# Both feed-forward down products: seven block products for eight in chunks of four K tiles, all low halves on GpSimd

## The chip, the cores and the metric

The kernel runs on one core of a Trainium2 chip. The metric is device time in microseconds of that core, from launch to end, as the median of several executions. Lower is better.

## The reference, cut to what matters

Two transformer-like blocks are applied to one sequence of 1024 tokens with 1024 features, all in fp32. Each block ends in a feed-forward. Only the two down projections matter here:

```
# first block: D_FF = 2816, 22 K tiles of 128
f = (gelu(gate) * val) @ w_down          # [1024, 2816] @ [2816, 1024]
h = h + rms_norm(f, ln_ffn_post)
# second block: D_FF_2 = 4096, 32 K tiles of 128
x = x + square(relu(h2 @ w_up_2)) @ w_down_2   # [1024, 4096] @ [4096, 1024]
return rms_norm_2(x, final_norm_2)
```

## The kernel before

Every fp32 product is made of three matmuls in TensorE's fp32r type. Each operand is rounded to a high half (ScalarE, `activation` Copy), the rest is taken as a low half (raw minus high, a `tensor_tensor` on GpSimd or VectorE), and TensorE adds high x high, high x low and low x high in PSUM. The low half is written over the raw data.

Five programs, one for each engine (SP issues the DMAs), are written out by hand in order. An engine runs its list strictly in order; semaphores hold it where it needs another's result. The class `Steps` (L107) numbers the steps of a repeated part, so that `wait(eng, name, j)` waits for step `name` of round `j`.

**First down product** (channels on the partitions, result `y[:, m, :]`, m = 0 to 7). It goes in 11 chunks of two K tiles. For each chunk SP loads 1 MB of `w_down` (L2612) and 1 MB of the stored activations (L2624), ScalarE rounds (L2633), GpSimd makes the low halves (L2646; those of the first activations are made by VectorE, L2659), TensorE makes 96 matmuls of 128x512 (`down_products`, L2670: eight output rows m, two PSUM banks each, two rows in flight), and VectorE adds each PSUM result to `y` (`add_one`, L2994; chunk 0 is copied by ScalarE, L2665). Three SBUF homes for chunks (L211) let the loads run ahead. The last chunk also feeds the sums of squares of the norm behind it.

**Second down product** (tokens on the partitions). It goes in 16 chunks of two K tiles in the same way (L2763, L2782, L2791, `token_products` L2691). `token_add` (L2723) scales each PSUM result by a per-token factor and adds it to `y` in one `scalar_tensor_tensor`. Behind chunks 0 and 1, TensorE transposes four residual tiles each into PSUM (L2705) and VectorE adds them (L2715). In the last chunk each output row is normed and stored.

Seven-product stages exist already in both up projections and in part of the second block's input projection (`r7_products`, L3128, called "ring" and "pair" stages): the two operands are cut into quadrants, VectorE makes the sums of quadrants, and seven block products replace eight. Those stages write their low halves on VectorE. SP, GpSimd, ScalarE, TensorE and VectorE reach the two down products in their programs at L3343 to L3356 and L3448 to L3462, L3539 to L3545 and L3570, L3664 to L3682 and L3785 to L3793, L3849 to L3852 and L3905 to L3912, L4027 to L4031 and L4161 to L4167.

Of the kernel before, what the change touches and what calls it, by code (L numbers as in the profile page):

```python
# [15 lines left out]
P = 128  # L16
T = 1024
# [61 lines left out]
DOWN1 = FF_TILES // 2  # L79
DOWN2 = FF2_TILES // 2  # L80
# [4 lines left out]
PRODUCT_OPENS = [True, True, False, True, False, False, False]  # L85
TILE_ORDER = [0, 4, 1, 5, 2, 6, 3, 7]
# [19 lines left out]

class Steps:  # L107
# [3 lines left out]
    def __init__(self, sem, names):  # L111
        self.sem, self.names, self.at = sem, names, 0
        self.index = {name: k for k, name in enumerate(names)}
        assert len(self.index) == len(names)

    def start(self, eng):
        eng.sem_inc(self.sem, len(self.names))
# [6 lines left out]
    def wait(self, eng, name, j):  # L124

        eng.wait_ge(self.sem, j * len(self.names) + (len(self.names) + self.index[name] + 1))
# [6 lines left out]
    def wait_iterations(self, eng, j):  # L133

        eng.wait_ge(self.sem, j * len(self.names) + len(self.names))


def build_program(nc, a, out):
    ctx = ExitStack()
    with ctx:  # L140
# [87 lines left out]
        token_sq = at("token_sq", 32, [P, D])  # L228
# [15 lines left out]
        def x7_hi_at(i, b0, b1):  # L244
            if len(x7_hi[i]) == 1:
# [22 lines left out]
        f2h = [[at("f2h_00", 76, [P, T], F32R), at("f2h_01", 88, [P, T], F32R)],  # L268
               [at("f2h_10", 168, [P, T], F32R), at("f2h_11", 172, [P, T], F32R)]]
        f2l = [at("f2l_0", 80, [P, 2, T], F32R), at("f2l_1", 160, [P, 2, T], F32R)]  # L270
        f2raw = [at("f2raw_0", 80, [P, 2, T]), at("f2raw_1", 160, [P, 2, T])]
        d2raw = [at("d2raw_0", 176, [P, 2, D]), at("d2raw_1", 152, [P, 2, D])]
        d2h = [at("d2h_0", 184, [P, 2, D], F32R), at("d2h_1", 144, [P, 2, D], F32R)]
        d2l = [at("d2l_0", 176, [P, 2, D], F32R), at("d2l_1", 152, [P, 2, D], F32R)]
# [354 lines left out]
        pre_sum = Steps(sem("pre_sum"), ["css", "cp"])  # L629
# [6 lines left out]
        sc_act = Steps(sem("sc_act"), ["tA0", "tA1"])  # L636
        sc_dve = Steps(sem("sc_dve"), ["SB00", "SB01", "SB10", "SB11", "SN0", "SN1"])
# [16 lines left out]
        out_pe = Steps(sem("out_pe"), ["tY0", "tY1", "gate0", "gate1"])  # L654
        out_act = Steps(sem("out_act"), ["square", "root", "ln0", "ln1", "hi"])
        out_dve = Steps(sem("out_dve"), ["sum", "mean", "center", "var", "rr", "norm", "gate0", "gate1"])
        out_pool = Steps(sem("out_pool"), ["lo"])
# [1950 lines left out]
        def down_home(c):  # L2608

            return 2 - c % 2 if c else 0  # L2610
# [1584 lines left out]
```

## Time and profile before

| what | value |
| --- | --- |
| time, median of 3 runs | 3028.42 us (3022.24 to 3031.68) |
| span of the profiled execution, first to last instruction | 3028.7 us |
| own time of that execution | one of the three runs' times; the page gives only its span |
| TensorE matmuls | 2909.7 us, 96% of the span |
| VectorE | 1822.3 us, 60% |
| ScalarE | 1191.0 us, 39% |
| GpSimd | 538.9 us, 18% |
| mean granted TensorE clock | 0.988 |

In the profile PE is TensorE, PEld its weight load, DVE VectorE, ACT ScalarE, POOL GpSimd, SPq the DMA queue of SP. L480 is the line of the matmuls of all three-matmul products outside the seven-product stages. A group's busy time adds the durations of its instructions. A matmul is shown with its whole length (389 ns), while the next starts before it ends, so the pace of matmuls is read from the length of a stretch and its count. "Idle before" says for what the engine waited before the instruction.

### The profile page before, as it was taken

How to read it: one execution, taken by the hardware profiler on the slowest of the kernel's cores; microseconds unless marked ns; L12 is line 12 of the kernel's file. 1: busy time of each engine (PE TensorE's matmuls, PEld its weight loads, DVE VectorE, ACT ScalarE, POOL GpSimd, SP SyncE). 2: the span in 40 equal slices, each digit the busy share in tenths (PEclk: the TensorE clock that was granted, in tenths of full speed). 3: DMA queues.
4: the chain of work that ended last, by engine and by line, in shares of the span. 5: the costliest groups of instructions: out<-in, count | busy, mean ns of one | idle time of the engine just before them, and what ended most of it. 6: DMA issues, size and time to landing. Idle time of an engine off the chain costs nothing.

```text
span 3028.7 us, 47692 instructions
## 1 busy us (share of the span) xinstructions
PE 2909.7 (96%) x20002; PEld 2338.6 (77%) x20002; DVE 1822.3 (60%) x2306; ACT 1191.0 (39%) x1769; POOL 538.9 (18%) x228
## 2 busy tenths in 40 slices
PE   8999988889899999999899999999899999999999
PEld 6877777777688888888688767666688888878887
DVE  3156778741799889444885455555456655554445
ACT  4155545632645555321543343444334333221112
POOL 3310122221100000444141200000021000043342
PEclk9999999999999999999999999999899999999999
DMA  6433430002422222322444634444544333342322
GB/s 210 152 114 112 126 114 25 27 32 78 159 70 84 84 84 77 133 111 84 132 149 147 208 105 126 147 135 136 195 132 132 105 112 111 125 160 84 112 84 111
DMA packets 252247, 350.09 MB, mean 116 GB/s; under 512 B 11377, under 2 KB 187642, under 8 KB 252034
## 3 DMA queue, kind: packets, MB, share of 16 engines
q1 hardware_dynamic: 237058, 299.85, 31.0%
q10 hardware_dynamic: 14976, 47.19, 4.1%
q8 instruction: 159, 2.61, 0.4%
q14 instruction: 54, 0.44, 0.0%
HBM read 238.17 MB, written 108.82 MB: 115 GB/s over the span
## 4 chain that ended last, share of the span: by engine, by line
PE 87%; DVE 5%; issue 3%; DMA 2%; ACT 2%; SPq 1%; POOL 0%; DVEq 0%; ACTq 0%
PE ps L480 36%; PE ps L3159 17%; PE ps L2929 10%; PE ps L2095 5%; PE ps L664 4%; PE ps L1512 4%; PE ps L2146 2%; PE ps L2165 2%; PE ps L2123 1%; PE ps L1575 1%; PE ps L2126 1%; DMA kl<-qk_lo 1%; PE ps L1553 0%; PE ps L506 0%; PE ps L2131 0%
## 5 line engine op out<-in xcount | busy, mean ns | idle before, releaser
L446 POOL TENSOR_TENSOR wl<-wraw,wh 128x1024 fp32r<-128x1024 f32 x62 | 157.2, 2537 | 1118.0 <-ACT wh L441 1108.4
L2734 DVE SCALAR_TENSOR_TENSOR y<-ps,token_s,y 128x1024 f32<-128x1024 f32 x120 | 154.0, 1284 | 164.1 <-PE ps L480 164.0
L480 PE MATMUL ps<-xh,wh 128*128 128x512 f32 x752 | 237.9, 398 | 5.4 <-DVE yb L1318 1.4
L480 PE MATMUL ps<-xl,wh 128*128 128x512 f32 x752 | 233.7, 392 | 0.0
L480 PE MATMUL ps<-xh,wl 128*128 128x512 f32 x752 | 233.2, 391 | 0.0
L441 ACT ACTIVATE wh<-wraw 128x1024 fp32r<-128x1024 f32 x78 | 82.4, 1058 | 268.1 <-PE ps L480 206.4
L480 PEld LDWEIGHTS ps<-xh,wh 128*128 128x128 f32 x752 | 139.8, 190 | 47.2 <-issue 9.4
L2996 DVE TENSOR_TENSOR y<-ps,y 128x1024 f32<-128x1024 f32 x79 | 96.8, 1225 | 125.6 <-PE ps L480 125.6
L2795 POOL TENSOR_TENSOR d2l<-d2raw,d2h 128x2048 fp32r<-128x2048 f32 x16 | 74.0, 4624 | 520.8 <-ACT d2h L2786 520.8
L480 PEld LDWEIGHTS ps<-xl,wh 128*128 128x128 f32 x752 | 142.4, 189 | 30.3
L480 PEld LDWEIGHTS ps<-xh,wl 128*128 128x128 f32 x752 | 142.3, 189 | 30.2
L480 PE MATMUL ps<-d2h,f2h 128*128 128x512 f32 x512 | 157.9, 389 | 0.0
L480 PE MATMUL ps<-d2l,f2h 128*128 128x512 f32 x512 | 157.6, 389 | 0.0
L480 PE MATMUL ps<-d2h,f2l 128*128 128x512 f32 x512 | 157.6, 389 | 0.0
L2359 DVE CUSTOM_DVE_ANT_0 pbuf<-ps,bias 128x640 f32<-128x640 f32 (+7 forms) x128 | 85.7, 706 | 99.5 <-PE ps L2131 47.2
L2650 POOL TENSOR_TENSOR d1l<-d1raw,d1h 128x2048 fp32r<-128x2048 f32 x11 | 50.9, 4627 | 490.8 <-ACT d1h L2639 490.8
L2786 ACT ACTIVATE d2h<-d2raw 128x2048 fp32r<-128x2048 f32 x16 | 30.7, 1921 | 255.4 <-DMA d2raw<-in_w_down 253.0
L3244 DVE SCALAR_TENSOR_TENSOR cb<-ub,cols,cb 128x1024 f32<-128x1024 f32 x88 | 112.5, 1299 | 5.1 <-ACT cb L3227 3.5
L480 PEld LDWEIGHTS ps<-d2l,f2h 128*128 128x128 f32 x512 | 96.1, 188 | 20.1
L480 PEld LDWEIGHTS ps<-d2h,f2h 128*128 128x128 f32 x512 | 96.1, 188 | 20.0
L480 PEld LDWEIGHTS ps<-d2h,f2l 128*128 128x128 f32 x512 | 96.1, 188 | 19.9
L2275 ACT ACTIVATE pt<-ps 128x512 f32<-128x512 f32 (+2 forms) x96 | 44.3, 465 | 166.8 <-PE ps L2146 166.8
(487 smaller groups left out, 7477.3 us busy)
## 6 DMA issues: line engine op xcount, KB each, us to landing
wraw<-in_w_in SPq DMA_DIRECT2D x48, 512.0 KB, 4.9
r_raw<-in_w_up SPq DMA_DIRECT2D x38, 512.0 KB, 3.8
residual<-src ACTq DMA_DIRECT2D x32, 512.0 KB, 5.0
w_raw<-in_w_up SPq DMA_DIRECT2D x32, 512.0 KB, 5.1
act_d<-act SPq DMA_DIRECT2D x32, 512.0 KB, 6.2
d2raw<-in_w_down SPq DMA_DIRECT2D x16, 1024.0 KB, 5.0
f2raw<-act_d SPq DMA_DIRECT2D x16, 1024.0 KB, 7.1
proj<-stage SPq DMA_DIRECT2D x30, 512.0 KB, 3.1
```

The lines of the kernel that those rows point to most:

```text
L441: nc.scalar.activation(wh[:, s, :, :], wraw[:, s, :, :], ACT.Copy).then_inc(w_hi, 1)
L446: nc.gpsimd.tensor_tensor(wl[:, s, :, :], wraw[:, s, :, :], wh[:, s, :, :].bitcast(F32), ALU.subtract).then_inc(w_lo, 1)
L480: mm = nc.tensor.matmul(ps[:, bank + h, :], w, x[:, h * HALF:(h + 1) * HALF], start=start and k == 0, stop=stop and k == 2)
L664: return nc.tensor.matmul(to, left, right, **kw)
L1512: ins = mm(ps[:, 2 * fill_slot(u) + h, :], w[:, s, kt, :], x[:, kt, h * HALF:(h + 1) * HALF], start=kt == 0 and part == 0, stop=kt == KT - ...
L2095: ins = mm(ps[:, 6 + h, :], w[:, s, kt, :], x[:, kt, h * HALF:(h + 1) * HALF], start=kt == 0 and part == 0, stop=kt == KT - 1 and part == 2)
L2359: a2_dve.done(nc.vector.tensor_tensor_reduce(pbuf[:, step % 3, m, 0:size], ps[:, 2 * m:2 * m + 2, :].rearrange("p a n -> p (a n)")[:, 0:size],
L2734: ins = nc.vector.scalar_tensor_tensor(out=y[:, m, :], in0=bank2(2 + m % 2), scalar=token_s2[:, m:m + 1], in1=y[:, m, :], op0=ALU.mult, op ...
L2929: mm = nc.tensor.matmul(ps[:, bank, :], w, x, start=PRODUCT_OPENS[b] and i == 0 and k == 0, stop=i == 3 and k == 2, skip_group_check=True)
L2996: nc.vector.tensor_tensor(y[:, m, :], bank2(2 + m % 2), y[:, m, :], ALU.add).then_inc(down_added, 1)
L3159: mm = nc.tensor.matmul(ps[:, bank, :], w, x, start=PRODUCT_OPENS[b] and i == 0 and k == 0, stop=i == 3 and k == 2, skip_group_check=True)
L3244: ff1_dve.done(nc.vector.scalar_tensor_tensor(out=cb[:, r, :], in0=ub[:, r, 2 - back:T + 2 - back], scalar=col("conv_w", (2 - back) * 2 * ...
```

## The change

The first down product becomes: two chunks of two K tiles as before (tiles 0 to 3), four chunks of four K tiles (tiles 4 to 19) with seven block products each, and one chunk of two (tiles 20 and 21). The second becomes: three chunks of two (tiles 0 to 5), six of four (6 to 29), one of two (30 and 31). Both residual turns move one chunk later.

A chunk of four K tiles is loaded as eight quarters of 512 KB. VectorE makes eight sums of two quarters each (128x1024). There are then seven left and seven right operands; ScalarE rounds each into a ring of three (first product) or four (second) slots, and GpSimd makes each of the fourteen low halves in place. TensorE makes 24 matmuls for each of seven block products, in four PSUM banks, alternating between the lower and upper four. Where `PRODUCT_OPENS` is false, a block product is accumulated on what the same four banks hold already. After each block product VectorE adds the four banks to one quadrant of `y`, in two halves: one 128x1024 `tensor_tensor` for a half in the first product, two 128x512 `scalar_tensor_tensor` in the second.

```diff
+DOWN1_TILES = [0, 2, 20]
+DOWN2_TILES = [0, 2, 4, 30]
+SUMS = {"T1": ("B3", "B12", "B0"), "S3": ("A4", "A0", "A21"), "T2": ("B2", "B5", "B3"), "T3": ("B4", "B5", "B12"),
+        "S1": ("A3", "A21", "A6"), "S2": ("A2", "A3", "A0"), "T4": ("B6", "B1", "B2"), "S4": ("A5", "A1", "A2")}
...
+        seven1 = Seven(0, 4, 4, lambda k, half: quarter_of(a["w_down"], k, half),
+                       lambda k, half: quarter_d(act1_d, k, half), *homes1, 3, False)
+        seven2 = Seven(4, 6, 6, lambda k, half: quarter_d(act2_d, k, half),
+                       lambda k, half: quarter_of(a["w_down_2"], k, half), *homes2, 4, True)
...
+        def seven_load(sp, g, e):
+            j, k, raw = g.first + e, g.tile0 + 4 * e, g.raw[e % 2]
+            if e:
+                d7_sum.wait(sp, "S1", j - 1)
+            if e >= 2:
+                d7_pe.wait(sp, "01", j - 2)
+            load("B0", g.right, 0, 0, 0)
+            load("B12", g.right, 0, 1, 0)
+            load("A0", g.left, 0, 0, 1)
+            load("A21", g.left, 0, 1, 1)
+            if e >= 2:
+                d7_pe.wait(sp, "11", j - 2)
+            load("B1", g.right, 1, 0, 2)
+            load("A1", g.left, 1, 0, 2)
+            if e >= 2:
+                d7_pe.wait(sp, "51", j - 2)
+            load("B5", g.right, 1, 1, 3)
+            if e >= 2:
+                d7_pe.wait(sp, "61", j - 2)
+            load("A6", g.left, 1, 1, 3)
...
+        def seven_round(act, g, e, b):
+            if b == 0:
+                d7_sum.wait(act, "S4", j)
+            if at_ >= g.ring:
+                d7_pe.wait(act, f"{(at_ - g.ring) % 7}1", g.first + (at_ - g.ring) // 7)
+            for x in "AB":
+                d7_hi.done(nc.scalar.activation(g.high[x][at_ % g.ring][:, :, :], g.raw[e % 2][f"{x}{b}"][:, :, :], ACT.Copy),
+                           f"{x}{b}")
...
+        def seven_lows_pool(pool, g, e):
+            for b in range(7):
+                seven_rest(pool, g, e, "A", b)
+                seven_rest(pool, g, e, "B", b)
...
+        def seven_products(pe, g, e):
+            for b in range(7):
+                d7_low.wait(pe, f"B{b}", j)
+                for h in range(2):
+                    if b >= 2:
+                        d7_add.wait(pe, f"{b - 2}{h}", j)
+                    elif e:
+                        d7_add.wait(pe, f"{b + 5}{h}", j - 1)
+                    for i in (2 * h, 2 * h + 1):
+                        for kt in range(2):
+                            for k, (w, x) in enumerate(((a_hi, b_hi), (a_hi, b_lo), (a_lo, b_hi))):
...
+        def seven_adds(dve, g, e, b):
+            for h in range(2):
+                d7_pe.wait(dve, f"{b}{h}", j)
+                if g.scaled:
+                    for i in range(2 * h, 2 * h + 2):
+                        ins = nc.vector.scalar_tensor_tensor(out=y[:, m, part], in0=ps[:, bank + i, :],
+                                                             scalar=token_s2[:, m:m + 1], in1=y[:, m, part],
+                                                             op0=ALU.mult, op1=ALU.add)
+                else:
+                    ins = nc.vector.tensor_tensor(to, ps[:, bank + 2 * h:bank + 2 * h + 2, :], to, ALU.add)
...
+        def seven_dve(dve, g):
+            names = list(SUMS)
+            for e in range(g.chunks):
+                for b in range(7):
+                    if e + 1 < g.chunks:
+                        if b < 4:
+                            seven_sums(dve, g, e + 1, names[2 * b:2 * b + 2])
+                    if b:
+                        seven_adds(dve, g, e, b - 1)
+                    elif e:
+                        seven_adds(dve, g, e - 1, 6)
+            seven_adds(dve, g, g.chunks - 1, 6)
... SP
+            seven_load(sp, seven1, 0)
             load_w(sp, U_FA, 0, w_cols(a["w_in_2"], FA_COL))
             load_w(sp, U_QKV2, 1, w_cols(a["w_in_2"], 0))
...
+            sp.wait_ge(down_done, 2 * KT)
+            for e in range(1, seven1.chunks):
+                seven_load(sp, seven1, e)
... VectorE, first product
+            p7_pe.wait(dve, "P4", F1_PAIRS - 1)
+            seven_sums(dve, seven1, 0, SUMS)
             dve.wait_ge(down_added, KT)
...
+            seven_dve(dve, seven1)
... VectorE, second product
+            for c in range(3):
                 for m in range(TT):
                     token_add(dve, c, m)
+                    if c == 1:
+                        seven_sums(dve, seven2, 0, list(SUMS)[m:m + 1])
... TensorE, first product
+            for c in range(2):
+                down_products(pe, c)
+            pe.wait_ge(down_added, 2 * KT)
+            for e in range(seven1.chunks):
+                seven_products(pe, seven1, e)
```

In the programs of ScalarE and GpSimd, the first chunk's rounding of the first product waits for down chunk 0 to be through TensorE, that of the second for token chunk 1. The two `wl` low halves that GpSimd makes for the next stage (L446) stand behind seven-chunk 1. In the second product SP issues the first chunk's eight quarters ahead of the residual's reload, and TensorE waits for the last residual addition and the last token addition before the first block product.

## Rows read from the trace of the kernel before

**Rows 1.** the page: busy time of each engine, share of the span; then the chain's shares.

```profile
PE 2909.7 (96%) x20002; PEld 2338.6 (77%) x20002; DVE 1822.3 (60%) x2306; ACT 1191.0 (39%) x1769; POOL 538.9 (18%) x228
...
PE 87%; DVE 5%; issue 3%; DMA 2%; ACT 2%; SPq 1%; POOL 0%; DVEq 0%; ACTq 0%
PE ps L480 36%; PE ps L3159 17%; PE ps L2929 10%; PE ps L2095 5%; PE ps L664 4%; PE ps L1512 4%; PE ps L2146 2%; PE ps L2165 2%; PE ps L2123 1%; PE ps L1575 1%; PE ps L2126 1%; DMA kl<-qk_lo 1%; PE ps L1553 0%; PE ps L506 0%; PE ps L2131 0%
```

**Rows 2.** chain that ended last, in time (start us, us, what), first down product.

```profile
1189.96 24.04 PE ps L3159 x106
...
1223.47 236.94 PE ps L480 x1044
1460.48 1.10 issue
```

**Rows 3.** the same chain, second down product.

```profile
2663.01 21.82 PE ps L480 x96
...
2689.81 21.83 PE ps L480 x96
...
2716.61 304.70 PE ps L480 x1344
...
3021.34 1.30 DVE y L2734
```

**Rows 4.** GpSimd in order of time (start us, us, instruction), chunk 4 of the first.

```profile
1295.78 4.63 POOL L2650 TENSOR_TENSOR d1l<-d1raw,d1h 128x2048 fp32r<-128x2048 f32 x1 [12.17 <-ACT d1h L2639]
1300.38 4.76 POOL L2656 TENSOR_TENSOR f1l<-f1raw,f1h 128x1024 fp32r<-128x1024 f32 x2
1305.10 4.74 POOL L446 TENSOR_TENSOR wl<-wraw,wh 128x1024 fp32r<-128x1024 f32 x2
```

**Rows 5.** one line's instructions: count, duration min/median/max in ns, first and last start.

```profile
L2996 DVE TENSOR_TENSOR y<-ps,y x79: 1224/1225/1225, 1248.3 to 1460.4; 128x1024 f32<-128x1024 f32 x79
...
L2734 DVE SCALAR_TENSOR_TENSOR y<-ps,token_s,y x120: 1277/1284/1285, 2692.6 to 3021.3; 128x1024 f32<-128x1024 f32 x120
...
L3191 DVE TENSOR_TENSOR ub<-r_u,r_m x19: 678/683/686, 875.8 to 1223.9; 128x512 f32<-128x512 f32 x19
...
L3193 DVE TENSOR_TENSOR ub<-ps,r_u x19: 680/693/693, 876.7 to 1224.4; 128x512 f32<-128x512 f32 x19
```

**Rows 6.** GpSimd and VectorE in order of time, where both read SBUF at 1216 us.

```profile
1216.50 4.61 POOL L2650 TENSOR_TENSOR d1l<-d1raw,d1h 128x2048 fp32r<-128x2048 f32 x1 [374.23 <-ACT d1h L2639]
...
1217.47 5.85 DVE L2663 TENSOR_TENSOR f1l<-f1raw,f1h 128x1024 fp32r<-128x1024 f32 x2 [4.60 <-ACT f1h L2644]
1223.25 0.68 DVE L3189 TENSOR_TENSOR ub<-ps,r_m 128x512 f32<-128x512 f32 x1
1223.85 0.68 DVE L3191 TENSOR_TENSOR ub<-r_u,r_m 128x512 f32<-128x512 f32 x1
...
1225.16 2.36 DVE L3204 TENSOR_TENSOR ub<-ub,rstd 128x1024 f32<-128x1024 f32 x2
```

**Rows 7.** the two engines again, 1523 to 1531 us.

```profile
1520.31 4.46 POOL L446 TENSOR_TENSOR wl<-wraw,wh 128x1024 fp32r<-128x1024 f32 x1
1524.79 4.39 POOL L2341 TENSOR_TENSOR ls<-st,hs 128x1024 fp32r<-128x1024 f32 x1
...
1522.42 1.19 DVE L2064 SCALAR_TENSOR_TENSOR st<-ps,rstd 128x1024 f32<-128x1024 f32 x1
1523.54 7.79 DVE L3033 TENSOR_TENSOR t_raw<-y,t_raw 128x2048 f32<-128x2048 f32 x2
```

**Rows 8.** a group of ScalarE's: busy us, mean ns of one.

```profile
L2644 ACT ACTIVATE f1h<-f1raw 128x1024 fp32r<-128x1024 f32 x20 | 20.1, 1053 | 7.6 <-DMA f1raw<-act_d 7.6
```

**Rows 9.** SP's DMA issues in order of time; GB/s in 40 slices of 2663:2690.

```profile
1234.17 0.33 SPq L3260 DMA_DIRECT2D act_d<-fout  x1
...
1267.31 0.37 SPq L2620 DMA_DIRECT2D d1raw<-in_w_down  x1
...
GB/s 0 115 97 400 431 407 401 267 267 194 279 328 419 431 413 413 437 413 376 376 431 401 431 431 401 425 425 413 395 419 425 407 188 49 97 309 449 407 407 449
```

**Rows 10.** the page: a 512 KB load's time from issue to landing.

```profile
proj<-stage SPq DMA_DIRECT2D x30, 512.0 KB, 3.1
```

**Rows 11.** stretches: busy us (x count) by engine, PEclk, DMA share, GB/s.

```profile
1733.50:1737.50 4.00, 0.58 (x3) 0.19 (x3) 1.23 (x1) 0.00 (x0) 0.00 (x0) 1.00 1.07 373
1738.00:1741.40 3.40, 3.40 (x13) 2.74 (x11) 0.00 (x0) 1.06 (x1) 1.33 (x1) 0.53 0.90 278
```

More of the change, by code:

```diff
@@ L104, with __init__, final @@
     t7: int
+@dataclass
+class Seven:
+    first: int
+    chunks: int
+    tile0: int
+    left: object
+    right: object
+    raw: list
+    low: list
+    high: dict
+    ring: int
+    scaled: bool
 class Steps:
-    def __init__(self, sem, names):
+    def __init__(self, sem, names, after=None):
         self.sem, self.names, self.at = sem, names, 0
+        self.shared = after is not None
+        self.base = after if self.shared else len(names)
         self.index = {name: k for k, name in enumerate(names)}
         assert len(self.index) == len(names)
+    def final(self, iterations):
+        return self.base + iterations * len(self.names)
     def start(self, eng):
+        assert not self.shared
         eng.sem_inc(self.sem, len(self.names))
@@ new lines, in seven_sums @@
+        def seven_sums(dve, g, e, names):
+            j, raw = g.first + e, g.raw[e % 2]
+            for name in names:
+                to, left, right = SUMS[name]
+                for group in {"T1": (0,), "S3": (1,), "T2": (3,), "T3": (0, 3), "S1": (1, 3), "T4": (2,), "S4": (2,)}.get(name, ()):
+                    dve.wait_ge(d7_loaded[group], 32 * (j + 2))
+                if name in ("T2", "S2", "T4", "S4"):
+                    d7_sum.wait(dve, {"T2": "T1", "S2": "S1", "T4": "T2", "S4": "S2"}[name], j)
+                if e >= 2:
+                    d7_pe.wait(dve, f"{to[1]}1", j - 2)
+                d7_sum.done(nc.vector.tensor_tensor(raw[to][:, :, :], raw[left][:, :, :], raw[right][:, :, :],
+                                                    ALU.add if name == "S1" else ALU.subtract), name)
@@ L3460, in _ @@
                 .then_inc(gain_loaded, 16)
-            for c in range(2, DOWN2):
-                load_token_chunk(sp, c)
+            load_token_chunk(sp, 2)
+            sp.wait_ge(rt_turned, KT)
+            for e in range(1, seven2.chunks):
+                seven_load(sp, seven2, e)
+            load_token_chunk(sp, DOWN2 - 1)
             for t in range(TT):
@@ L3569, in _ @@
                 split_lo(pool, n, n % 2)
-            for c in range(DOWN2):
+            for c in range(DOWN2 - 1):
                 split_token_lo(pool, c)
+            for e in range(seven2.chunks):
+                seven_lows_pool(pool, seven2, e)
+            split_token_lo(pool, DOWN2 - 1)
         @block.scalar
@@ L3850, in _ @@
             e1_dve.wait(pe, "c12", F1_PAIRS - 2)
-            for c in range(DOWN1):
-                down_products(pe, c, behind=c == DOWN1 - 1)
+            for c in range(2):
+                down_products(pe, c)
+            e1_act.wait(pe, "c21", F1_PAIRS - 1)
+            e1_dve.wait(pe, "c12", F1_PAIRS - 1)
+            pe.wait_ge(down_added, 2 * KT)
+            for e in range(seven1.chunks):
+                seven_products(pe, seven1, e)
+            d7_add.wait(pe, "51", seven1.first + seven1.chunks - 1)
+            down_products(pe, DOWN1 - 1, behind=True)
             post_sums_pe(pe, 24, KT - 2)
@@ L4160, in _ @@
             pair_squares(dve, PAIRS2 - 1, 1)
[L4161 removed]
+            p7_pe.wait(dve, "P4", PAIR0 + PAIRS2 - 1)
+            for c in range(3):
                 for m in range(TT):
                     token_add(dve, c, m)
[L4164 to L4165 removed]
+                    if c == 1:
+                        seven_sums(dve, seven2, 0, list(SUMS)[m:m + 1])
+                if c:
+                    for kt in range(4 * c - 4, 4 * c):
                         add_residual(dve, kt)
+            dve.wait_ge(rt_added, KT)
+            dve.wait_ge(down_added, TOKEN0 + 3 * TT)
+            seven_dve(dve, seven2)
+            d7_add.wait(dve, "61", seven2.first + seven2.chunks - 1)
             last_token_add(dve, DOWN2 - 1)
```

230 lines of the change are left out of this document (156 added, 74 removed).

## The prediction

> **What bounds the kernel now.** I read the shares of the page first. TensorE is busy 96% of the span, and 87% of the chain that ended last is TensorE, 36% on line 480 alone, which holds both down products [rows 1]. Next the chain in order of time. The first down product runs from 1223.47 us as one piece, 1044 matmuls in 236.94 us, then a short tail [rows 2]. The second runs as 96, 96 and 1344 matmuls in 21.82, 21.83 and 304.70 us [rows 3]. So the pace is 0.227 us for a 128x512 matmul, and nothing but TensorE holds these stages. The seven-product stage ahead of them has the same pace, 106 in 24.04 us [rows 2]. Whatever leaves TensorE here shortens the end one for one, until another engine can't follow. The question is who has to follow, so I then read GpSimd and VectorE instruction by instruction.
>
> **Removed.** A pair of old chunks is 192 matmuls, 192 x 0.227 = 43.6 us. A new chunk is 7 x 24 = 168, 38.1 us, 5.45 us for each block product. Ten new chunks would give back 10 x 5.45 = 54.5 us if nothing else held them.
>
> **GpSimd.** Five lows of 1024 elements or their like run back to back from 1295.78 to 1309.84 us: 4.60 for the wide one, then four at 2.36 [rows 4]. Fourteen make 33.0 us for a chunk, within 38.1. A low that had been held and is released takes 2.27 (below).
>
> **VectorE.** Its eight sums read two SBUF operands. Two such instructions of 1024 columns, with no low beside them, take 2.36 us (line 3204 [rows 6]); half of it, and a little less for one behind another, is 1.13. The additions read PSUM and SBUF: 1.225 us for 1024 columns, so two in 2.3 us for a block product of the first down product [rows 5]. The scaled 512-column form is not in the trace. Its bounds are 0.60 (the unscaled one's pace [rows 6]) and 1.28 (the full-width scaled one [rows 5]). I take 0.67, the unscaled plus the 0.06 us by which the scaled exceeds the unscaled at 1024; four make 2.7 us. Together 9 + 16 or 19 us for a chunk: by busy time VectorE fits too.
>
> **The two together do not fit.** At 1216.50 GpSimd starts a low that ends at 1221.11. VectorE's `f1l`, which reads two SBUF tiles, starts at 1217.47; two of them take 5.85 us where two unhindered take 2.36. They end at 1223.32, so the first can only have run after 1221.1, in about 1.1 us [rows 6]. At 1523.54 it goes the other way and back: low `wl` ends at 1524.77, VectorE's first `t_raw` runs, then the low `ls`, started at 1524.79, ends only at 1529.18, and the second `t_raw` ends at 1531.33 [rows 7]. The lengths are 2.15 (VectorE, 2048 wide) and 2.27 (low), alternately: total exclusion, in turns. Additions from PSUM feel nothing: 199 of them stay within 1.224 to 1.225 and 1.277 to 1.285 us [rows 5], with lows beside many of them. For a held sum of 1024 columns I take 1.09, half of 2.15 rounded up.
>
> So in `seven_dve`, where two sums stand ahead of each of four additions, VectorE must let a low pass between the two sums, and GpSimd's next lows run while it adds. For the second down product one step is: sum 1.09, low 2.27, sum 1.09; then the additions of 2.7, in which one low (2.27) ends and the next has begun; the next sum waits that out, so two lows, 4.6 us. The step takes 9.05 us against TensorE's 5.45. TensorE may be two block products ahead of the additions, no more. Followed through a chunk from the start of its product 0: the additions of the previous product 6 end at 5.3, T2 runs to 8.4, a low to 10.6, T3 to 11.7, the first half addition to 13.1; product 2 begins at 13.3 instead of 10.9, 2.4 late. S1, low, S2 and the addition end at 22.1; product 3 begins 3.6 after product 2 has ended. By the last pair GpSimd has run out of rounded operands, since the next chunk is rounded only after S4; product 4 waits 1.4. The other products follow without a gap. Sum 7.4: a chunk takes 45.5 us, 1.9 more than the 43.6 it replaces.
>
> **Second down product, sum.** Sums of the first chunk stand between the additions of token chunk 1, and T2 meets chunk 2's wide low (4.6 us): about 3.5 us late in all. Ahead of the first block product TensorE waits for the last residual addition, 1.4. Chunks: 46.0 + 4 x 45.5 + 38.1 (the last has no sums beside it) = 266.1 against 261.4, + 4.7. Together + 9.6.
>
> **First down product, sum.** SP can issue the first chunk's quarters at 1234.6, behind the store that it issued at 1234.17 [rows 9]. A 512 KB load lands after 3.1 us [rows 10]; in a row they follow at 512 KB over some 400 GB/s [rows 9], 1.3 to 1.4 us. The eighth lands at about 1247, six of eight sums follow until 1254, and only then the first addition of down chunk 1, which TensorE needs at 1250.7: 4.4 us late. The new wait for the last addition of chunk 1 costs 1.4. With rounding this is + 6.2. Chunk 1's eight loads are issued only when down chunk 1 is done (its home overlaps), so the last lands some 11.4 us into seven-chunk 0, while T2 and T3 stand ahead of the addition that product 2 needs at 10.9: T2, a low, T3, addition, so product 2 starts near 17.4 and the chunk takes 44.9. In the two middle chunks the additions are 2.26 us, just a low's length: if VectorE comes back before GpSimd has taken its next low, a step is 6.7, else 9.05. That gives 41.3 to 47.1 us for each (the upper with the two `wl` lows in one of them, 4.7). Between these I take 44.5. The last is 38.1. Sum 172.0 against 174.3, with the 6.2: + 3.9; ends 0 and + 8.
>
> **Others.** ScalarE rounds fourteen in 14 x 1.05 = 15 us for a chunk [rows 8]: hidden behind TensorE's 38, and if that cover were gone it would add about 1 us ahead of each low. The loads are 4 MB for each 45 us, as before; from the third chunk on they are issued a whole chunk ahead. Their cover is gone only in the place priced above. The residual's reload, put behind 4 MB more, is needed 27 us later than before; nothing. The two last chunks of two tiles are loaded and split a chunk ahead; nothing, at most the 1.4 of one addition. The new gaps of 2.4 and 3.6 us may lower TensorE's clock: before a stretch of 3.4 us at 0.53 of the clock it had done 0.58 us of work in 4.0 [rows 11], so the idle part was 3.4 us. Such a stretch (the 1.2 GHz level) costs 1.7 us. In the middle steps VectorE is later than TensorE anyway; I take 1 us in all, at most 8 x 1.7 = 14.
>
> **Sum.** 3.9 + 9.6 + 1.0 = 14.5. On the profiled execution's span of 3028.7 that is 3043; its span is 0.3 us from the median of the runs, and its own time is among the three, so I set the same 3043 against the median of 3028.42.
>
> **Rivals.** A: the exclusion holds but the pairs of sums slip through together, or the additions do, so that only GpSimd's total binds: 14 x 2.36 + 8 x 1.09 = 41.8 us for a chunk. Then the second product is 4.9 + 2.4 - 5 x 1.8 - 5.5 = -7, the first 6.2 + 1.3 - 2 x 1.8 - 5.5 = -2: 3020. For it: 2.3 us of additions is so close to a low. Against it: the low between the two `t_raw` [rows 7]. The Trainium skill, "SBUF — State Buffer", section "Who interferes with whom", says that issue order decides who blocks, and for the whole instruction; read so, the waiting low was issued ahead of the second sum, and A could not come about in the second product. The trace agrees in the one place shown, and A's chance is set from that place.
>
> B: the sums do not hold GpSimd, nor it them. Then steps are below 5.45 and chunks 38.1, but for the first loads: -10 and -26 us, 2992. Against it is every held instruction above.
>
> C: the slower side. TensorE's lower clock falls on the path at every gap. It is idle over 3 us once in each of the eight chunks with sums beside them, and where 1.7 us is not hidden each time, the sum is 14.5 + 13 = 3056. It decides once the half-clocked block product ends later than VectorE's addition two before it, a margin of 1.4 to 3.6 us.
>
> D: the change does not do what it says: the matmul count would be unchanged and the time that of before. The code counts 168 a chunk; no chance of note.
>
> **How the numbers follow.** Forecast 0.54 (own range 3034 to 3051), A 0.18, B 0.08, C 0.17, rest 0.03. The range goes from 3018 to 3060: it takes A's upper half, the forecast and most of C. A measurement of this kernel tells 0.3%, 9 us, from no change. Faster (under 3019.3) is B and half of A, 0.17. Within: half of A and a tenth of the forecast and the rest, 0.17. Slower: 0.66.
>
> **What would show it.** VectorE's sums beside lows with a mean near 3 us instead of 1.22, in the same stretches lows over 2.4; block products 2 and 3 of a chunk started by VectorE's `y`, gaps of 2 to 4 us there; chunks near 45.5 us in the second product, the last 38; 240 matmuls fewer; GpSimd's busy share up by some 10 points. It is wrong if sums beside lows stay at 1.22, if a chunk in the middle takes under 42 us, or if the wait there ends on a low instead of on `y`.

## The result, and the profile after

The changed kernel takes 3060.35 us (median of 4 runs, 3058.9 to 3065.2); the kernel before, run beside it, 3027.78. The ratio is 1.0113, 95% interval 1.0098 to 1.0127: slower, by 32.6 us. I had forecast slower, 3043, with a range that ended at 3060, 0.35 us below what came. The direction was right, and so was the exclusion between the two engines; the size forecast, 14.5 us, was less than half. The profiled execution has a span of 3063.4 us, 34.7 more than before.

The page's busy time of each engine, then the shares of the chain that ended last, by engine and by line:

```profile
PE 2882.0 (94%) x19762; PEld 2307.8 (75%) x19762; DVE 1985.6 (65%) x2450; ACT 1250.6 (41%) x1849; POOL 728.4 (24%) x308
...
PE 79%; DVE 8%; DMA 4%; issue 4%; POOL 2%; ACT 2%; SPq 1%; DVEq 0%; ACTq 0%
```

Against [rows 1] TensorE has 240 matmuls fewer, as the diff says, yet its share fell to 94% and its part of the chain from 87% to 79%. What took its place is VectorE, DMA and GpSimd. Where, the chain in order of time says (start us, us, what), here the first down product, which answers to [rows 2]:

```profile
1237.95 10.77 DMA v_raw_A<-in_w_down
...
1249.89 1.22 DVE v_raw_B L3333
...
1256.96 18.99 PE ps L529 x72
...
1279.90 9.90 DMA v_raw_A<-in_w_down
...
1293.17 3.35 DVE v_raw_B L3333
...
1297.80 24.48 PE ps L3377 x96
...
1323.44 3.47 POOL v_low_A L3351
...
1390.44 60.43 PE ps L3377 x264
```

L3333 is a sum, L3351 a low half, L3377 the matmuls of a block product, L3400 and L3395 the additions of the first and second product. Before, one piece of 236.94 us of matmuls stood here. A sum that waits for a low half is held inside its own instruction, so its length (3.35 at 1293.17) holds that wait. Now the chain leaves TensorE three times: for the eighth load of the first chunk and the sums behind it, for the eighth load of chunk 1 with T2 and T3 (names of two sums) behind it, and for a long row of GpSimd's low halves.

The stretches of the two products (us; busy us and count of PE, PEld, DVE, ACT, POOL; granted clock, DMA share, GB/s). The first row is the two short chunks up to the first block product, then the four chunks of the first product, then the short chunks and both turns of the second, then its six chunks:

```profile
1222.09:1277.46 55.37, 46.48 (x192) 37.52 (x193) 30.49 (x26) 20.57 (x20) 24.48 (x9) 0.91 0.41 143
1277.46:1327.54 50.08, 40.88 (x168) 33.36 (x169) 31.92 (x22) 12.06 (x12) 29.49 (x12) 0.90 0.44 156
1327.54:1371.30 43.76, 38.79 (x169) 31.12 (x167) 37.90 (x25) 17.97 (x18) 43.76 (x16) 1.00 0.32 108
1371.30:1412.62 41.32, 40.40 (x168) 32.64 (x169) 30.12 (x19) 12.06 (x12) 41.32 (x16) 0.96 0.00 1
1412.62:1450.70 38.08, 38.08 (x169) 31.54 (x168) 17.14 (x14) 15.33 (x15) 35.40 (x15) 1.00 0.15 56
2676.18:2758.37 82.19, 74.38 (x354) 62.13 (x352) 54.23 (x41) 16.15 (x15) 39.58 (x14) 0.98 0.46 173
2758.37:2808.87 50.50, 40.92 (x169) 33.32 (x169) 34.77 (x34) 12.05 (x12) 29.68 (x12) 0.90 0.45 156
2808.87:2856.76 47.89, 41.95 (x169) 33.53 (x168) 43.13 (x37) 14.06 (x14) 38.99 (x15) 0.93 0.25 88
2856.76:2902.52 45.76, 40.29 (x170) 32.54 (x169) 42.17 (x37) 14.06 (x14) 38.52 (x15) 0.96 0.27 93
2902.52:2948.01 45.49, 40.00 (x170) 32.42 (x168) 42.14 (x37) 14.06 (x14) 38.50 (x15) 0.96 0.27 93
2948.01:2996.03 48.02, 42.09 (x169) 33.59 (x168) 40.81 (x37) 14.06 (x14) 38.98 (x15) 0.93 0.03 11
2996.03:3034.11 38.08, 38.08 (x169) 31.54 (x168) 19.75 (x28) 11.74 (x11) 28.97 (x12) 1.00 0.15 56
```

A pair of old chunks is 43.6 us. The two last chunks, with no sums beside them, give back the full 5.5 us each, and one in the middle (41.3) 2.3 of them. Chunk 1 of the first (43.8) comes out even, and everything else costs. First to last matmul, the first down product takes 250.5 us against 239.7 (+10.9) and the second 379.9 against 358.4 (+21.4); the other 2.4 us lie outside both, part of it in longer stretches of lower clock at 1477 and 1750 us, in work that no edit touches.

### The profile page after: what moved, and what is told of

It reads as the page before. It is cut to its first block, busy times and chain, and to the rows that moved or that the text cites. A ratio compares the mean times of both kernels' runs of the same rounds, so it can differ in the third digit from the quotient of the medians.

```text
span 3063.4 us, 47721 instructions
## 1 busy us (share of the span) xinstructions
PE 2882.0 (94%) x19762; PEld 2307.8 (75%) x19762; DVE 1985.6 (65%) x2450; ACT 1250.6 (41%) x1849; POOL 728.4 (24%) x308
## 4 chain that ended last, share of the span: by engine, by line
PE 79%; DVE 8%; DMA 4%; issue 4%; POOL 2%; ACT 2%; SPq 1%; DVEq 0%; ACTq 0%
PE ps L529 20%; PE ps L3232 16%; PE ps L3001 9%; PE ps L3377 9%; PE ps L2144 5%; PE ps L713 4%; PE ps L1561 4%; PE ps L2195 2%; PE ps L2214 2%; PE ps L2172 1%; DMA kl<-qk_lo 1%; POOL v_low_B L3351 1%; POOL v_low_A L3351 1%; DVE v_raw_A L3333 1%; PE ps L1624 1%
## 5 line engine op out<-in xcount | busy, mean ns | idle before, releaser
L3377 PE MATMUL ps<-v_highB,v_highA 128*128 128x512 f32 x560 | 226.4, 404 | 50.3 <-DVE y L3395 32.4
L3377 PE MATMUL ps<-v_low_B,v_highA 128*128 128x512 f32 x560 | 224.2, 400 | 0.0
L3377 PE MATMUL ps<-v_highB,v_low_A 128*128 128x512 f32 x560 | 223.7, 400 | 0.0
L3344 ACT ACTIVATE v_highA<-v_raw_A 128x1024 fp32r<-128x1024 f32 x70 | 74.2, 1060 | 345.0 <-PE ps L3377 315.5
L3351 POOL TENSOR_TENSOR v_low_A<-v_raw_A,v_highA 128x1024 fp32r<-128x1024 f32 x70 | 185.3, 2647 | 109.1 <-ACT v_highA L3344 109.1
L3351 POOL TENSOR_TENSOR v_low_B<-v_raw_B,v_highB 128x1024 fp32r<-128x1024 f32 x70 | 192.4, 2748 | 0.0
L3377 PEld LDWEIGHTS ps<-v_highB,v_highA 128*128 128x128 f32 x560 | 109.2, 195 | 80.5 <-issue 51.2
L3395 DVE SCALAR_TENSOR_TENSOR y<-ps,token_s,y 128x512 f32<-128x512 f32 x168 | 115.4, 741 | 43.8 <-PE ps L3377 43.8
L3377 PEld LDWEIGHTS ps<-v_highB,v_low_A 128*128 128x128 f32 x560 | 108.9, 194 | 23.7
L3377 PEld LDWEIGHTS ps<-v_low_B,v_highA 128*128 128x128 f32 x560 | 108.9, 195 | 22.5
L2713 POOL TENSOR_TENSOR d1l<-d1raw,d1h 128x2048 fp32r<-128x2048 f32 x3 | 13.8, 4617 | 388.0 <-ACT d1h L2702 388.0
```

The lines of the kernel that those rows point to most:

```text
L3351: d7_low.done(nc.gpsimd.tensor_tensor(g.low[e % 2][name][:, :, :], g.raw[e % 2][name][:, :, :], g.high[x][(7 * e + b) % g.ring][:, :, :].b ...
L3377: mm = nc.tensor.matmul(ps[:, bank + i, :], w[:, kt, cut], x[:, kt, :], start=PRODUCT_OPENS[b] and kt == 0 and k == 0, stop=kt == 1 and k ...
L3395: ins = nc.vector.scalar_tensor_tensor(out=y[:, m, part], in0=ps[:, bank + i, :], scalar=token_s2[:, m:m + 1], in1=y[:, m, part], op0=ALU. ...
```

## The experiments

Chunk lengths below are from the same view as above, written in order: four of the first product, six of the second. Those of the changed kernel are 50.1, 43.8, 41.3, 38.1 and 50.5, 47.9, 45.8, 45.5, 48.0, 38.1. The kernel before has a median of 3026.6 to 3026.7 us beside these runs. A difference from the changed kernel (3060.35) joins two intervals and is good to some 5 to 7 us. A hole is the time from the end of one matmul to the start of the next, where TensorE stood.

**Sums that read one operand (e1_no_pair_read).** The sums are left out. In the place of each stand a reduction of one quarter and a constant fill.

```diff
-                d7_sum.done(nc.vector.tensor_tensor(raw[to][:, :, :], raw[left][:, :, :], raw[right][:, :, :],
-                                                    ALU.add if name == "S1" else ALU.subtract), name)
+                nc.vector.tensor_reduce(raw[to][:, :, 0:1], raw[left][:, :, :], AX_X, ALU.add)
+                d7_sum.done(nc.vector.memset(raw[to][:, :, 1:HALF], 0.5), name)
```

> Leaves the eight sums of a chunk out: each is replaced by a tensor_reduce over the left operand (one SBUF input, 1024 columns) and a memset of the target (no input), so VectorE works at least as long but never reads two SBUF operands. Theory (total exclusion between a two-operand SBUF read of VectorE's and a low of GpSimd's, in turns): lows stay at 2.4 us, the middle chunks of the second down product go from 45.5 to 48 us down to 38 to 40.5, those of the first from 43.8 and 41.3 to 38 to 39; chunk 0 of each still waits for its loads but no longer for lows, 44 to 46 instead of 50. Sum about 3060 - 49 = 3011 us. Rival (VectorE simply has too much work between two additions): chunks stay at 45 us or grow, 3060 or more. Rival (the loads are late): all chunks as in the changed kernel, 3060.

Measured: 3028.81 us, ratio 1.0013 (1.0003 to 1.0023). Chunks 47.7, 39.5, 39.3, 38.1 and 49.4, 39.9, 39.8, 39.8, 39.8, 38.1. Groups of GpSimd's and VectorE's instructions from 2758 us on (busy us, mean ns of one, idle before them), first of the changed kernel, then of this one:

```profile
L3351 POOL TENSOR_TENSOR v_low_B<-v_raw_B,v_highB 128x1024 fp32r<-128x1024 f32 x38 | 106.7, 2807 | 0.0
...
L3333 DVE TENSOR_TENSOR v_raw_B<-v_raw_B,v_raw_B 128x1024 f32<-128x1024 f32 x10 | 26.6, 2655 | 2.7 <-DMA v_raw_A<-act_d 2.7
```

```profile
L3351 POOL TENSOR_TENSOR v_low_B<-v_raw_B,v_highB 128x1024 fp32r<-128x1024 f32 x38 | 91.3, 2403 | 0.0
...
L3334 DVE MEMSET v_raw_A<- 128x1022 f32 x20 | 18.2, 910 | 3.2 <-issue 3.2
L3333 DVE TENSOR_REDUCE v_raw_B<-v_raw_B 128x2 f32<-128x1024 f32 x15 | 18.0, 1199 | 5.5 <-DMA v_raw_A<-act_d 5.5
```

What stands in for a sum takes 2.1 us, more than an unheld sum (1.22) and less than a held one (3.1 to 3.4), but runs at its own length, and the low halves beside it too (2.40 us). The middle chunks of the second product fall from 45.5 to 48.0 us to 39.8. So the stall of the middle chunks is the exclusion between two-operand reads and low halves, not VectorE's amount of work. The time in all missed the expectation of 3011 by 18 us: chunk 0 took 47.7 and 49.4 where 44 to 46 were expected, and the two short chunks ahead of the first took 60.6 (53.9 in the changed kernel), since more VectorE time stood ahead of the first addition. That points at the order behind the loads, and the next two runs look at that.

**Chunk 0's sums two block products later (e2_late_first).**

```diff
                     if e + 1 < g.chunks:
-                        if b < 4:
-                            seven_sums(dve, g, e + 1, names[2 * b:2 * b + 2])
+                        plan = (('0022220', '2222000') if g.scaled else ('0022220', '2222000'))[e > 0]
+                        at_ = sum(map(int, plan[:b]))
+                        seven_sums(dve, g, e + 1, names[at_:at_ + int(plan[b])])
```

A digit of the plan is the number of sums ahead of one block product's additions.

> Only in chunk 0 of each product, the pairs of sums for chunk 1 stand two steps later (ahead of additions 1 to 4, after the loads have landed). Theory (chunk 0 is long because T2 and T3, ahead of addition 0, wait for the eighth load of chunk 1, and because the gap of 9 us brings 10 us of TensorE at 1.2 GHz): chunk 0 goes from 50.1 and 50.5 to about 41.5 us, the 10.2 us stretches go, chunk 1 of the second stays at 47 to 48; sum -13 to -18, 3042 to 3047. Rival (the exclusion alone makes chunk 0 long, the pairs cost the same wherever they stand): chunk 0 above 46, total above 3052.

Measured: 3047.02, ratio 1.0075 (1.0056 to 1.0093), 13.3 us less than the changed kernel. Chunks 39.7, 46.7, 41.3, 38.1 and 40.7, 48.7, 45.7, 48.1, 48.1, 38.1. This run's chunk 0 of either product:

```profile
1274.98:1314.71 39.73, 38.75 (x169) 31.28 (x169) 35.16 (x22) 11.96 (x12) 32.83 (x11) 1.00 0.55 196
...
2745.00:2785.69 40.69, 38.49 (x168) 31.56 (x169) 36.29 (x34) 11.85 (x12) 24.89 (x9) 1.00 0.54 193
```

The loads are issued as late (from 1.5 and 1.3 us ahead of the chunk), but nothing that TensorE needs stands behind them, and the clock stays at 1.00 where it was 0.90. Ten us of either chunk 0 were a wait for loads, carried by VectorE's order, and the slow clock behind it. Some 3 us come back later in each product: in the first in chunk 1, where GpSimd is busy without a pause, in the second mostly in chunk 3, which now behaves as chunks 1 and 4 do (why, in the next section).

**The first chunk's sums between additions (e3_first_between).** Two sums ahead of the eight additions of the last short chunk and two behind each of the first three, instead of all eight ahead; in the second product all eight are done behind the sixth addition of the last short chunk before the turn, not behind the eighth.

```diff
-            seven_sums(dve, seven1, 0, SUMS)
+            seven_sums(dve, seven1, 0, list(SUMS)[:2])
             dve.wait_ge(down_added, KT)
             for m in range(KT):
                 add_one(dve, 1, m)
+                if m < 3:
+                    seven_sums(dve, seven1, 0, list(SUMS)[2 * m + 2:2 * m + 4])
...
-                        seven_sums(dve, seven2, 0, list(SUMS)[m:m + 1])
+                        at_ = (0, 2, 4, 5, 6, 7, 8, 8, 8)
+                        seven_sums(dve, seven2, 0, list(SUMS)[at_[m]:at_[m + 1]])
```

> Only the sums of each product's chunk 0 are moved: in the first product T1 and S3 ahead of the additions of down chunk 1 and a pair behind each of its additions 0, 1, 2; in the second 2, 2, 1, 1, 1, 1 behind the additions 0 to 5 of token chunk 1. Theory (6 sums ahead of the first addition cost 7.4 us and 2.6 us of half clock; T4 and S4 meet the wide low of token chunk 2 and cost 5.5 at the turn): the two down chunks go from 53.9 to about 45 us, the turn from 10.5 to about 5.5; sum -12 to -15, 3045 to 3048. Rival (the eighth load is what the first product waits for, and later sums make the first lows late): the gap only moves to the first block product, total within 3 us of 3060.

Measured: 3046.57, ratio 1.0070 (1.0055 to 1.0085), 13.8 less than the changed kernel. The short chunks of the first product take 45.56 us instead of 53.85, the turn of the residual 7.5 instead of 10.5 (5.5 were expected); the chunks are within 0.8 us of the changed kernel's. So of the gap at 1249 us and the slow clock behind it, 8.3 us were the six sums in a row behind the loads. The row is the short chunks:

```profile
1220.40:1265.96 45.56, 44.64 (x192) 35.64 (x192) 29.33 (x25) 20.60 (x20) 18.72 (x7) 1.00 0.50 172
```

**One sum at a time (e4_one_a_step).** The same edit as for late sums, with the plan `'1111220'` for every chunk.

> The same eight sums, spread as 1, 1, 1, 1, 2, 2, 0 over the seven steps of a chunk instead of 2, 2, 2, 2. Theory (a step with one sum needs no low between two sums: 1.09 + two lows 4.6 = 5.7 us against 9.05): chunks 40.5, 40.5, 40.8 and 38.1 us in the first product, 39 to 42.5 in the second; sum -35 to -42, 3018 to 3025. Rival (VectorE's total work, or GpSimd's total of lows and held time, binds): the chunks keep 43.8 and 45.5 us, only chunk 0 gains from its later sums, 3045 to 3055.

Measured: 3019.32, ratio 0.9978 (0.9968 to 0.9987), 41 us less than the changed kernel. Chunks 38.4, 46.6, 40.6, 38.1 and 39.4, 41.6, 43.9, 40.6, 42.3, 38.1. In the middle chunks of the second product the same eight sums and fourteen low halves, of which only the order differs, cost 40.6 to 43.9 us where pairs cost 45.5 to 48.0. A single sum ahead of an addition waits out one low half, a pair two. In the first product the gain is all in chunk 0. Its chunks 1 and 2 take 87.2 us together (85.1 with pairs; I had expected 81.3), and GpSimd is busy for all of it. So there the rival holds: GpSimd's low halves and their waits are the limit, and the order of sums doesn't help. In chunk 3 of the second product they ran almost back to back too, 38.4 of 40.6 us busy:

```profile
2871.39:2912.02 40.63, 38.36 (x169) 31.45 (x168) 40.15 (x35) 13.86 (x14) 38.38 (x15) 1.00 0.30 104
```

**Seven of the fourteen low halves on VectorE (e5_vlow).** Sums stay where the change put them.

```diff
             for b in range(7):
                 seven_rest(pool, g, e, "A", b)
-                seven_rest(pool, g, e, "B", b)
...
...
+        def seven_v_low(dve, g, n):
+            e, b = divmod(n, 7)
+            if e < g.chunks and b in V_LOWS:
+                j, name = g.first + e, f"B{b}"
+                d7_hi.wait(dve, name, j)
+                d7_vlow.done(nc.vector.tensor_tensor(g.low[e % 2][name][:, :, :], g.raw[e % 2][name][:, :, :],
+                                                     g.high["B"][n % g.ring][:, :, :].bitcast(F32), ALU.subtract), name)
...
                     elif e:
                         seven_adds(dve, g, e - 1, 6)
+                    if e or b:
+                        seven_v_low(dve, g, 7 * e + b - 1 + g.ring)
```

> Edit: the seven right-hand low halves of a chunk are made by VectorE between its additions, so GpSimd makes seven of fourteen and VectorE seven. Sums stand where they stand in the changed kernel. Theory (the cost of a pair of sums is the low halves of GpSimd that pass between them, so that fewer of them pass when GpSimd has fewer to make): middle chunks of the first product near 38.1 (changed kernel 41.3 to 43.8), of the second near 41 (changed kernel 45.5 to 48.0), chunk 0 of either stays near 48 to 50 since its loads and sums come late whatever GpSimd does. About 12 us less in the first product and 18 to 22 in the second: 3028 to 3034. Rival 1 (VectorE has too much to do: 8 sums, 7 lows and the additions come to 9 + 8 + 16 to 19 us, plus what it is held): chunks stay over 44 and the time is 3050 to 3065. Rival 2 (GpSimd's total of 33 us is what binds, as TensorE waits for its lows): chunks drop to 38.1 in both products, 3015 to 3022.

Measured: 3030.49, ratio 1.0022 (1.0012 to 1.0032), 29.9 less than the changed kernel. Chunks 48.2, 38.1, 42.7, 38.1 and 48.0, 41.3, 41.3, 41.3, 41.3, 38.1. Chunk 0 stays near 48 and the second product's middle chunks fall to 41, both as expected; chunk 1 of the first falls to 38.1, but chunk 2, at 42.7, does not: a hole of 2 us ahead of its product 4 was followed by 3.4 us of lower clock. The rival of an overloaded VectorE, chunks over 44, falls, and in e6_all below VectorE does the same work in chunks of 38.1. Here it is busy 41.30 of 41.33 us, which includes its waits:

```profile
2794.85:2836.18 41.33, 38.62 (x170) 31.38 (x169) 41.30 (x44) 14.07 (x14) 18.02 (x7) 1.00 0.30 102
```

**The order edits together, without and with that (e7_order, e6_all).** Both have the first sums between additions and later, spread sums: plans `'0112220'` and `'0022220'` for chunk 0 and the later ones of the first product, `'0222200'` and `'1122200'` of the second. e7_order leaves the low halves on GpSimd, e6_all puts seven on VectorE. Unlike what the expectation of e6_all says, the last plan does put one sum ahead of each of the first two additions.

> Three edits together: the right-hand low halves on VectorE (as in the run beside this), the first chunk's sums spread between additions of the last short chunk, and the sums of later chunks moved one or two block products later (fewer at a time, none ahead of the first two additions). If the causes found so far are all of the excess (late first sums, chunk 0's loads, held pairs, half clock behind the gaps), then chunk 0 takes 39 to 42 us, the others 38.1 to 39, the starts lose 3 to 5 us and the turn 2 to 3: 2985 to 2998, faster than the kernel before. Rival (the later sums leave ScalarE and GpSimd too little time ahead of the next chunk's first block product, so the wait moves there): a gap of 2 to 4 us at each chunk's start, 3005 to 3020.

> The order edits of the run beside this alone (first sums between additions, later sums moved and spread), all fourteen low halves still on GpSimd. Theory: chunk 0 at 39.5 to 41, other chunks of the first product 40 to 43 and of the second 41 to 45 (as in the runs with one sum a step and with late sums): 3003 to 3015, and what the move of low halves to VectorE is worth with a good order is the distance to the run beside it, 12 to 20 us. Rival (order alone removes all waits; the place of the lows is nothing): both runs within 3 us of each other.

Measured: e7_order 3017.41, ratio 0.9972 (0.9961 to 0.9984); e6_all 2991.47, ratio 0.9889 (0.9875 to 0.9902), 35 us faster than the kernel before and 69 faster than the changed one. e7_order ended 2.4 us above its range: its chunks are 38.5, 44.9, 42.2, 38.1 and 44.3, then 42.0 to 42.6, 38.1. Of e6_all the chunks are 38.2, 40.9, 38.1, 38.1 and 43.1, then 38.1 five times; its two starts still lost 6.5 and 5.8 us, more than the 3 to 5 that I expected. Its chain through the chunks of 38.1 of the second product, then VectorE and GpSimd in order of time inside one of them:

```profile
2745.71 214.10 PE ps L3395 x936
```

```profile
2822.43 1.21 DVE L3371 TENSOR_TENSOR v_low_B<-v_raw_B,v_highB 128x1024 fp32r<-128x1024 f32 x1
2823.56 1.21 DVE L3337 TENSOR_TENSOR v_raw_A<-v_A,v_raw_A 128x1024 f32<-128x1024 f32 x1
2824.81 1.23 DVE L3337 TENSOR_TENSOR v_raw_A<-v_raw_A,v_raw_A 128x1024 f32<-128x1024 f32 x1
2825.95 2.72 DVE L3413 SCALAR_TENSOR_TENSOR y<-ps,token_s,y 128x512 f32<-128x512 f32 x4
...
2819.55 2.60 POOL L3355 TENSOR_TENSOR v_low_A<-v_raw_A,v_highA 128x1024 fp32r<-128x1024 f32 x1 [3.03 <-ACT v_highA L3348]
2824.99 3.32 POOL L3355 TENSOR_TENSOR v_low_A<-v_raw_A,v_highA 128x1024 fp32r<-128x1024 f32 x1 [2.85 <-ACT v_highA L3348]
```

Three two-operand instructions of VectorE run in a row, none held, because GpSimd has no second low half waiting. TensorE runs 936 matmuls as one piece. The rival of e6_all, a new gap at each chunk's start, didn't come. The rival of e7_order falls too: with the same order, the place of seven low halves is worth 26 us, where 12 to 20 were expected. The gains don't add up: e7_order is e4_one_a_step with another plan and the first sums moved (13.8 us by themselves), and yet its 2 us less are within the intervals. Its first start is shorter by 8.4 us, but chunks 0 to 4 of the second product take 213.2 us together for 207.7. No run joins the plan of e4_one_a_step with the other edits.

## Why the forecast had the sign and not the size

**Where it was right.** The step of the second product, followed product by product, is in the trace. Forecast: product 2 starts at 13.3 us of the chunk, product 3 starts 3.6 us after product 2 has ended, product 4 waits 1.4. In the chunk from 2902.52 the matmuls of product 2 start at 13.24, product 3 comes 3.55 late and product 4 1.5; the chunk is 45.5 as forecast. The last of the three is not a wait: product 3 took 6.92 us instead of 5.44 at a lower clock, and VectorE's addition was ready 0.3 us before it ended. So here the clock was hidden behind VectorE but for 0.3 us, as I had said. VectorE and GpSimd in order of time, in that chunk:

```profile
2914.21 2.72 DVE L3395 SCALAR_TENSOR_TENSOR y<-ps,token_s,y 128x512 f32<-128x512 f32 x4
2916.84 3.12 DVE L3333 TENSOR_TENSOR v_raw_A<-v_A,v_raw_A 128x1024 f32<-128x1024 f32 x1
2919.99 3.28 DVE L3333 TENSOR_TENSOR v_raw_A<-v_raw_A,v_raw_A 128x1024 f32<-128x1024 f32 x1
2923.20 2.71 DVE L3395 SCALAR_TENSOR_TENSOR y<-ps,token_s,y 128x512 f32<-128x512 f32 x4
...
2916.47 2.41 POOL L3351 TENSOR_TENSOR v_low_A<-v_raw_A,v_highA 128x1024 fp32r<-128x1024 f32 x1
2918.82 3.37 POOL L3351 TENSOR_TENSOR v_low_B<-v_raw_B,v_highB 128x1024 fp32r<-128x1024 f32 x1
```

From one addition to the next is 8.99 us (9.05 forecast): two sums whose length of 3.12 and 3.28 is mostly waiting, and additions at 0.68 a piece of 512 columns (0.67 forecast). The ends show the turns: a low at 2918.88, the first sum 1.08 later, the next low at 2922.19, 2.23 later, the second sum 1.08 later. I had read 1.09 and 2.27 from [rows 6, 7]. The Trainium skill, "SBUF — State Buffer", section "Who interferes with whom", names the pair (VectorE with two SBUF inputs, GpSimd) and has issue order decide who blocks. The trace agrees on the pair; of the order it shows that a GpSimd instruction enters between two VectorE sums that stand back to back, each time one is waiting.

**The steps that failed** are three: the clock was put at 1 us, the cover of the loads was said to be gone in one place only, and T2 was let run free. In traces against traces it is 34.7 us where 14.5 were forecast (the chunks of seven products replace 174.3 and 261.4 us, the last of each is 38.1 in both columns, and rounding leaves 0.3):

| term | forecast | measured |
| --- | --- | --- |
| first product: start | +6.2 | +11.8 (55.4 for 43.6) |
| first product: chunk 0 | 44.9 | 50.1 |
| first product: two middle chunks | 89.0 | 85.1 |
| second product: start | +4.9 | +6.8 |
| second product: chunk 0 | 46.0 | 50.5 |
| second product: chunks 1 to 4 | 182.0 | 187.2 |
| clock, on top | +1.0 | some 12.5, in the rows above |
| elsewhere | 0 | +2.4 |

*Loads.* I had the eighth quarter of the first chunk landed 12.4 us after the first was issued. It was issued at 1233.16, the eighth was there at 1248.7: 15.6 us for 4 MB, 270 GB/s in the mean, so 3.2 us more. In chunk 0 it was 13.9 us (1275.97 to 1289.83), a us later than in my sum. In most of that time the queue did move near the 400 GB/s that I took; what I left out are the first 3 us, in which it moves 0 to 340 GB/s, a later dip to 297, and ahead of the first chunk a store of 0.5 MB. Everything on VectorE's list waits behind the eighth, so this goes on the path whole.

In the second product I had no late load at all: "their cover is gone only in the place priced above". But SP issues chunk 1's quarters only behind the last turn of the residual (L2782), for which it waits 42.8 us; then the chain goes over the eighth:

```profile
SPq L3301 <- PE ps L2782: 42.8, 1, 42.8
...
2757.08 0.37 SPq L3301
...
2760.70 10.73 DMA v_raw_A<-act_d
```

It lands 13 us into chunk 0, product 2 starts at 20.8 us of the chunk instead of some 13, and with the slow clock behind that hole this outweighs the two later waits that then don't come: 50.5 for 46.0.

*T2 held.* In chunk 0 I let T2 run free when its operand lands. It met a low half and took 3.41 us, then T3 3.35, instead of 1.1 and some 3.4; product 2 began 20.3 us into the chunk and not 17.4.

*The clock.* This is the largest miss: I took 1 us in all, since VectorE would be the later one anyway. It was so in chunks 2 and 3 of the second product, but not for three long holes of 7.4, 9.2 and 9.6 us. Stretches of lower clock that begin inside them, at 1251.8, 1292.7 and 2774.1, and run on when TensorE works again:

```profile
1251.80:1262.00 10.20, 5.04 (x12) 3.97 (x13) 6.21 (x6) 5.79 (x6) 5.00 (x3) 0.50 0.01 2
...
1292.70:1302.90 10.20, 5.10 (x12) 4.11 (x13) 10.16 (x8) 0.00 (x0) 2.74 (x1) 0.50 0.17 45
...
2774.10:2784.30 10.20, 5.18 (x12) 4.12 (x13) 10.17 (x11) 0.00 (x0) 2.47 (x1) 0.50 0.16 50
```

The clock is at its 1.2 GHz level for 10.2 us each time; TensorE works in the later half, at half pace, and loses 2.5 us on the path. Three times that is some 7.6 us. A long hole and the clock behind it are one cost: in the run with late first sums both went.

*The second product's chunks 1 and 4.* Forecast 45.5, measured 47.9 and 48.0. A further low half gets between T4 and S4. VectorE and GpSimd in chunk 1:

```profile
2832.18 1.78 DVE L3333 TENSOR_TENSOR v_raw_B<-v_raw_B,v_raw_B 128x1024 f32<-128x1024 f32 x1
2833.88 3.41 DVE L3333 TENSOR_TENSOR v_raw_A<-v_raw_A,v_raw_A 128x1024 f32<-128x1024 f32 x1
...
2830.48 2.40 POOL L3351 TENSOR_TENSOR v_low_A<-v_raw_A,v_highA 128x1024 fp32r<-128x1024 f32 x1 [1.94 <-ACT v_highA L3344]
2832.84 3.38 POOL L3351 TENSOR_TENSOR v_low_B<-v_raw_B,v_highB 128x1024 fp32r<-128x1024 f32 x1
```

In chunks 2 and 3 this pair of low halves is over before S4, which takes 1.21. The difference begins with the clock. Product 2 and product 4 of chunk 1, then product 2 of chunk 3 as stretches, and the rounding of operand 6, which waits until product 2 is through and frees one of the four slots, in chunks 1 and 3:

```profile
2822.10:2829.20 7.10, 7.09 (x24) 5.50 (x24) 7.07 (x4) 0.00 (x0) 6.44 (x3) 0.78 0.25 74
2838.76:2845.90 7.14, 7.14 (x25) 5.74 (x26) 5.22 (x8) 0.57 (x1) 4.44 (x2) 0.76 0.01 2
2915.75:2921.30 5.55, 5.55 (x24) 4.40 (x24) 5.52 (x4) 0.00 (x0) 5.55 (x3) 1.00 0.07 11
...
2829.35 1.06 ACT L3344 ACTIVATE v_highA<-v_raw_A 128x1024 fp32r<-128x1024 f32 x1 [7.40 <-PE ps L3377]
...
2921.49 1.06 ACT L3344 ACTIVATE v_highA<-v_raw_A 128x1024 fp32r<-128x1024 f32 x1 [5.90 <-PE ps L3377]
```

In chunk 1 the clock fell behind the hole of 2.2 us ahead of product 2, and the product took 7.0 us for 5.5. ScalarE's rounding came 20.48 us into the chunk for 18.97, GpSimd's low halves as much later, and one of them then stood between T4 and S4, so that product 4 started 0.7 us later. The clock fell once more at the hole ahead of product 4, where nothing hides it: 1.7 us. Together 2.4, in chunk 4 likewise. The twelve such chunks of this kernel and of the two runs above that keep the pairs agree: the seven with product 2 at the lower clock took 47.9 to 48.7 us, the five with it at full clock 45.5 to 45.8. Why the clock falls behind some holes of 2.2 us and not behind others stays open, and no run changes the clock alone.

So the clock cost 7.6 and 4.9, some 12.5 us. Rival C had this mechanism with 1.7 us at all eight chunks, 13 us and 3056; its sum was near, with the cost in other places.

*The turn.* Chunk 2's low halves `d2l` and `f2l` hold T4 for 4.04 us and S4 for 2.17, so from the last matmul ahead of the first turn to the next chunk's first it is 10.5 us for 5.1, 5.4 more. I had 3.5 for it, with the wide low half at T2, not at T4; with the sums done earlier it was 7.5.

*The middle of the first product* was cheaper than forecast. The chain there runs over GpSimd's low halves back to back, busy 43.76 of 43.76 and 41.32 of 41.32 us. That is rival A's rule, fourteen of 2.36 and eight passes of VectorE at 1.09, 41.8 us. In that product the additions are short enough that VectorE is back in time and GpSimd's total binds; I had named this as the lower end and taken a value between. A chunk under 42 us, and a wait that ends on a low half, were two of my own signs of being wrong; for the first product they came, and the account by held pairs on VectorE doesn't hold there. That its four chunks sum to 173.3 us where I had 172.0 is luck: I had put chunk 0 too short and the middle too long. My ends for this product, 0 and +8, don't follow from 41.3 and 47.1 either, which give -2.5 and +9.1; it came to +10.9, outside both. GpSimd's busy share rose by 6 points, not 10.

Rival B falls with every held sum, D with the 240 matmuls that are gone.

## What to carry to other kernels

Two engines that exclude each other are not to be added up by busy time; write down whose instruction is waiting when the other ends, and give the engine on TensorE's path at most one such instruction at a time, or take the other engine's waiting work away. The first helped in the second product only; where GpSimd was the limit, only the second did (chunks 1 and 2 of the first product took 44.9 and 42.2 us in e7_order, 40.9 and 38.1 in e6_all). An in-order engine that serves TensorE must not have an instruction that waits for a fresh load ahead of one that TensorE needs: here such sums at two starts and two first chunks cost some 27 us, 13.8 and 13.3 in the two runs that moved them. A stall behind which the clock falls is to be priced with the slow stretch, and with what that makes late on the other engines.

## What the runs showed of the hardware that I had not expected

- `tensor_reduce` (one SBUF operand, 1.20 us) and `memset` (0.91 us) of 1024 columns on VectorE run at their own length beside GpSimd's low halves, and those at 2.40 us; only VectorE's two-operand reads held and were held.
- Holes of 7.4 to 9.6 us each brought 10.2 us at the 1.2 GHz level, half of it still inside the hole; holes of 1.7 to 3.3 us in the second product 3.4 us or none: of the four of 2.2 us ahead of product 2, two.
- Eight 512 KB loads in a row took 13.9 to 15.6 us until the last had landed, 270 to 300 GB/s in the mean though the queue reached 400; the page's median for another group of 512 KB loads is 3.0 us from issue to landing.
- The same low half (1024 columns) takes 1.21 us on VectorE unheld and 1.67 in the mean among GpSimd's, against 2.40 on GpSimd. Moving seven of a chunk to the engine that was already the busier of the two made all four middle chunks of the second product shorter.
